# Expert rows weighted on leaving PSUM and added to the residual in DRAM by an accumulating scatter

## The chip, the cores and the metric

The kernel runs on one core of a Trainium2 chip. A core has five engines with queues of their own: TensorE (PE; its weight loads are shown as PEld), VectorE (DVE), ScalarE (ACT), GpSimd (POOL) and SyncE (SP). They meet through semaphores. Sixteen DMA engines serve the core. The metric is the device time of one execution in microseconds.

## What is computed

Two transformer blocks follow each other on 1024 tokens of width 1024, all in float32. The change lies at the seam between them: the mixture of experts that ends the first block, and the two norms behind it.

```
weight = p_group[:, None] * jax.nn.softmax(top_l, axis=-1)          # 2 experts of 32 per token
expert = (g_sel[:, None] * EXPERTS_PER_GROUP + top_i).astype(jnp.int32)
...
y = (jax.nn.silu(xb @ w_gate[e]) * (xb @ w_up[e])) @ w_down[e]      # for each expert's rows
out[token] += y * weight                                            # both rows of a token
...
x = x + hierarchical_moe(rmsnorm(x, norm2_g), ...)                  # residual
return rmsnorm(x, final_g)                                          # end of the first block
```

The second block begins with another norm of that result and its projections to queries, keys, values and a pooled branch.

## The kernel before

**Routing** (`route`). VectorE works out for each token its two experts, its place in the expert's list and its two weights `pair_w` (128 tokens by 2 slots by 8 tiles). Sixteen small matmuls of 0/1 matrices (`at_row`, `in_block`) turn these into lists, one column for each of 55 blocks of 88 rows. Adding 1024 for pairs of the second slot gives two lists from one: `row_ids` (tokens to gather) and `out_ids` (rows of a DRAM array `expert_rows` of 2048 rows, one for each pair of token and slot). GpSimd gathers block 0 within this stage, and VectorE splits two more weight units there. A barrier ends the stage.

**Experts** (`experts`). 32 blocks run, one for each expert; blocks 33 to 55 are for experts with over 88 rows, and none of them runs with these inputs. The weights of a block are 6 units of 1 MB, which SyncE loads into 13 raw slots; a slot is free again when its unit has been split. ScalarE copies a unit to reduced precision (`expert_high`), VectorE takes the remainder (`expert_rest`), both into 4 slots, and TensorE makes each product in three passes. The block's output leaves `y_ps` in two halves, one by ScalarE (`left`) and one by VectorE (`right`), into one of two `y_rows` slots. GpSimd issues for each block the gather of a block three ahead and then the store of this one, an indirect scatter to `expert_rows`; rows beyond the list's end are skipped by a bounds check. The last four raw slots lie in `res`, the place of the residual; the residual itself waits in DRAM as `mixed_residual`, and when those slots are done SyncE loads it back in 8 loads (L1781). At the end SyncE waits for the last stores and loads the first two tiles of `expert_rows`.

**Combination and norms** (first part of `project_second`). For each of 8 tiles of 128 tokens, VectorE adds the two expert rows with their weights to `res` (`put_together`, L2354), ScalarE squares and sums (L2268, L2270), VectorE scales (`final_norm`), ScalarE squares again, VectorE scales again into `poolT` (`next_norm`), TensorE transposes (L2208), and ScalarE and VectorE copy the transposed tile out of PSUM in a high part and a rest. ScalarE and VectorE also split the first four weight tiles of the projections (`ring`). From tile 3 to tile 6 TensorE runs a quarter of the first projections behind each tile's transposes. The order on each engine is written out by hand in the loops over t; the loads of `expert_rows` go through four buffers.

Of the kernel before, what the change touches and what calls it, by code (L numbers as in the profile page):

```python
# [14 lines left out]
ALU = mybir.AluOpType  # L15
# [1389 lines left out]
class CombinedRows:  # L1405


    BUF = 4

    def __init__(self, m):  # L1410
        self.m = m
        self.y = m.mixT2[:].rearrange("p (b s) d -> p b s d", s=2)
        self.y_in = [m.sem(f"y_in{i}") for i in range(self.BUF)]

    def load(self, sp, t):
        for slot in range(2):
            at = slot * SEQ + t * P
            sp.dma_start(self.y[:, t % self.BUF, slot, :], self.m.y_dram[at:at + P, :]).then_inc(self.y_in[t % self.BUF], 16)

# [19 lines left out]
def route(nc, m, A, router, weights, rows):  # L1439
# [3 lines left out]
    with ExitStack() as mem:  # L1443
# [37 lines left out]
        second = sb("second_slot", [CAP, BLOCKS])  # L1481
# [10 lines left out]
        list_mm = sem("row_list_mm")  # L1492
        ids_done = sem("row_ids_done")
# [10 lines left out]
        def _(pe):  # L1504
# [13 lines left out]
            last.then_inc(list_mm, 1)  # L1518

# [18 lines left out]
        def _(dve):  # L1538
# [22 lines left out]
            for slot in range(2):  # L1561
                step(nc.vector.tensor_scalar(place[:, slot, :], router.tokens[:], float(slot * SEQ - NOWHERE), None, ALU.add))
# [33 lines left out]
            def picked(out, table):  # L1596
# [44 lines left out]
            step(nc.vector.tensor_tensor(m.pair_w[:, 0, :], diff[:], pg[:], ALU.mult))  # L1641
            step(nc.vector.tensor_tensor(m.pair_w[:, 1, :], m.pair_w[:, 0, :], ratio[:], ALU.mult))
# [19 lines left out]
def experts(nc, m, A, weights, taken):  # L1662
# [3 lines left out]
    with ExitStack() as mem:  # L1666
# [16 lines left out]
        out_idx = sb("block_out_ids", [CAP, 1], I32)  # L1683
# [18 lines left out]
        res_back = sem("residual_back")  # L1702
# [52 lines left out]
        def left(act, s):  # L1755
            nc.scalar.activation(y[:, s, 0:BANK], ps_y[0:CAP, 0, :], ACT.Copy).then_inc(y_left, 1)

        def right(dve, s):
            nc.vector.tensor_copy(y[:, s, BANK:D], ps_y[0:CAP, 1, :]).then_inc(y_right, 1)  # L1759
# [13 lines left out]
        def _(sp):  # L1773
# [22 lines left out]
            sp.wait_ge(res_back, 16 * TT)  # L1796
# [6 lines left out]
        def put_rows(pool, s, ids):  # L1803

            pool.indirect_dma_start(m.y_dram, bass.IndirectOffsetOnAxis(ap=ids, axis=0), y[:, s, :], None,  # L1805
                                    bounds_check=2 * SEQ - 1, oob_is_err=False).then_inc(y_out[s], 16)

        @block.gpsimd
        def _(pool):
# [12 lines left out]
            for b in range(EXPERTS):  # L1822
                if b + R < EXPERTS:
                    gather(b + R)
                store(b)
            def over(j):
                pool.wait_ge(x_turned, j + EXPERTS)
                nc.gpsimd.tensor_copy(idx[:], m.row_ids[:, bass.ds(j + EXPERTS, 1)]).then_inc(over_idx, 1)
                pool.wait_ge(y_out[0], (j + EXPERTS // S) * 16)
                nc.gpsimd.tensor_copy(out_idx[:], m.out_ids[:, bass.ds(j + EXPERTS, 1)]).then_inc(over_idx, 1)  # L1830
                pool.wait_ge(over_idx, j * 2 + 2)
# [1803 lines left out]
```

## Time and profile before

| | |
|---|---|
| median of 3 runs | 2582.94 us (2579.58 to 2583.18) |
| the profiled execution | 2580.04 us, span 2578.2 us |
| granted TensorE clock, mean | 0.964 of full speed |
| busy: TensorE, VectorE, ScalarE, GpSimd | 93%, 61%, 41%, 16% |
| routing | 526 to 564 us |
| experts | 564 to 1147 us |
| combination, norms, first quarters of the projections | 1150 to 1218 us |

The page of the profile gives busy time by engine, the span in 40 slices, the DMA queues and the costliest groups of instructions. Its averages mix stages with different limits, so the stages are read apart. The traffic of GpSimd's indirect transfers is on a queue of its own (`software_dynamic`), that of SyncE's loads on another.

### The profile page before, as it was taken

The page shows a single profiled execution, that of the slowest core. Times are in us where ns is not written, and L with a number is a line of the kernel's source. Part 1 is how long each engine was busy: PE and PEld are TensorE (multiplying, and loading weights), DVE is VectorE, ACT ScalarE, POOL GpSimd, SP SyncE. Part 2 cuts the span into 40 slices and gives each one's busy share as a digit, 9 for nine tenths or more (in the row PEclk, how much of TensorE's full clock was granted, in tenths as well). Part 3 has the DMA queues.
Part 4 walks back from the last instruction along what each step waited for, and adds up shares of the span by engine and source line. Part 5 has one row for each costly group of instructions (what it writes and reads, how often), then busy time and mean ns, then how long its engine had stood idle before and what let it go on. Part 6 is the DMA issues. An engine that isn't in the chain of part 4 may idle for free. (4 is left out here: it accounts for less than half of the span.)

```text
span 2578.2 us, 28488 instructions
## 1 busy us (share of the span) xinstructions
PE 2401.0 (93%) x11160; PEld 1826.6 (71%) x11160; DVE 1581.1 (61%) x1702; ACT 1064.2 (41%) x1281; POOL 400.7 (16%) x280
## 2 busy tenths in 40 slices
PE   7999988939999999966999999998969999999998
PEld 6776556826666666646776778887858888887787
DVE  5552675368999999958213652223589998874444
ACT  4221122237777777745213741113344434433322
POOL 3110101011222222210300210000033232310000
PEclk9999998969999999987999999999989999999999
DMA  5121041289999999966310011113212222226343
GB/s 161 41 64 53 18 171 48 82 303 350 373 386 380 373 376 375 368 253 221 95 49 17 2 50 49 49 49 131 82 41 83 90 89 83 82 78 228 123 161 137
DMA packets 192965, 397.27 MB, mean 154 GB/s; under 512 B 17270, under 2 KB 120694, under 8 KB 176456
## 3 DMA queue, kind: packets, MB, share of 16 engines
q1 hardware_dynamic: 183624, 378.76, 41.5%
q0 software_dynamic: 9216, 16.80, 2.1%
q8 instruction: 83, 1.36, 0.2%
q14 instruction: 42, 0.34, 0.0%
HBM read 357.75 MB, written 47.18 MB: 157 GB/s over the span
## 5 line engine op out<-in xcount | busy, mean ns | idle before, releaser
L1398 DVE TENSOR_TENSOR expert_rest<-expert_raw,expert_high 128x2048 fp32r<-128x2048 f32 x135 | 306.0, 2290 | 43.6 <-ACT expert_high L1392 41.8
L1392 ACT ACTIVATE expert_high<-expert_raw 128x2048 fp32r<-128x2048 f32 x135 | 257.9, 1913 | 23.8 <-PE expert_up_ps L143 8.5
L141 PE MATMUL up_ps<-blocks_high,up_operand_high 128*128 128x512 f32 x616 | 241.8, 393 | 14.4 <-DVE plain_blocks_rest L3013 11.7
L143 PE MATMUL up_ps<-blocks_high,up_operand_rest 128*128 128x512 f32 x616 | 241.1, 391 | 0.0
L1805 POOL DMA_INDIRECT expert_rows<-y_rows,out_ids x32 | 85.2, 2662 | 424.6 <-DVE y_rows L1759 424.6
L141 PE MATMUL down_ps<-w_down_high,prod_high 128*128 128x512 f32 x352 | 138.4, 393 | 8.1 <-DVE w_down_rest L185 8.1
L141 PEld LDWEIGHTS up_ps<-blocks_high,up_operand_high 128*128 128x128 f32 x616 | 116.6, 189 | 40.4 <-issue 16.2
L3230 DVE TENSOR_TENSOR up_operand_rest<-res,up_operand_high 128x512 fp32r<-128x512 f32 x154 | 143.0, 940 | 3.0 <-ACT up_operand_high L3186 3.0
L1398 DVE TENSOR_TENSOR expert_rest<-res,expert_high 128x2048 fp32r<-128x2048 f32 x57 | 129.6, 2291 | 15.3 <-ACT expert_high L1392 14.7
L142 PE MATMUL down_ps<-w_down_rest,prod_high 128*128 128x512 f32 x352 | 137.9, 392 | 0.0
L142 PE MATMUL up_ps<-plain_blocks_rest,up_operand_high 128*128 128x512 f32 x352 | 137.8, 391 | 0.0
L143 PE MATMUL down_ps<-w_down_high,prod_rest 128*128 128x512 f32 x352 | 137.7, 391 | 0.0
L143 PEld LDWEIGHTS up_ps<-blocks_high,up_operand_rest 128*128 128x128 f32 x616 | 116.5, 189 | 24.3
L3144 POOL TENSOR_TENSOR res<-res 128x512 f32<-128x512 f32 x22 | 30.7, 1397 | 619.7 <-DVE plain_blocks_rest L3013 393.3
L3186 ACT ACTIVATE up_operand_high<-res 128x512 fp32r<-128x512 f32 x154 | 89.2, 622 | 83.8 <-PE up_ps L143 64.3
L1392 ACT ACTIVATE expert_high<-res 128x2048 fp32r<-128x2048 f32 x57 | 109.4, 1919 | 9.5 <-PE expert_up_ps L143 5.1
L141 PE MATMUL expert_gate_ps<-expert_high,x_high 128*88 128x512 f32 x256 | 104.0, 406 | 2.0 <-DVE x_rest L1745 2.0
L141 PE MATMUL y_ps<-expert_high,hid_high 128*88 128x512 f32 x256 | 102.5, 400 | 1.9 <-DVE y_rows L1759 1.9
L3441 DVE TENSOR_TENSOR prod_rest<-res,prod_high 128x512 fp32r<-128x512 f32 x44 | 30.5, 692 | 119.9 <-ACT prod_high L3414 119.9
L141 PE MATMUL gates_ps<-hT_high,gates_w_high 128*128 128x512 f32 x256 | 100.5, 393 | 3.3 <-DVE gates_w_rest L185 3.3
L142 PE MATMUL up_ps<-mixed_blocks_rest,up_operand_high 128*128 128x512 f32 x264 | 103.2, 391 | 0.0
L142 PE MATMUL expert_gate_ps<-expert_rest,x_high 128*88 128x512 f32 x256 | 102.2, 399 | 0.0
(432 smaller groups left out, 5915.4 us busy)
## 6 DMA issues: line engine op xcount, KB each, us to landing
expert_raw<-in_w_down_dram SPq DMA_DIRECT2D x46, 1024.0 KB, 19.0
expert_raw<-in_w_up_dram SPq DMA_DIRECT2D x45, 1024.0 KB, 19.7
expert_raw<-in_w_gate_dram SPq DMA_DIRECT2D x44, 1024.0 KB, 17.8
res<-in_w_up_dram SPq DMA_DIRECT2D x88, 256.0 KB, 4.0
res<-in_w_down_dram SPq DMA_DIRECT2D x44, 512.0 KB, 4.1
res<-in_w_gate_dram SPq DMA_DIRECT2D x20, 1024.0 KB, 22.2
res<-in_w_in_dram SPq DMA_DIRECT2D x38, 512.0 KB, 4.4
res<-in_w_up_dram SPq DMA_DIRECT2D x19, 1024.0 KB, 20.2
```

The costliest lines, as they stand in the source:

```text
L141: nc.tensor.matmul(out, w_high, x_high, start=start, stop=False)
L142: nc.tensor.matmul(out, w_high, x_rest, start=False, stop=False)
L143: return nc.tensor.matmul(out, w_rest, x_high, start=False, stop=stop)
L1392: self.nc.scalar.activation(self.high_part[:, n % SPLIT_SLOTS, :], self.raw[n % RAW_SLOTS], ACT.Copy) \
L1398: self.nc.vector.tensor_tensor(self.rest_part[:, s, :], self.raw[n % RAW_SLOTS], self.high_part[:, s, :].bitcast(F32), ALU.subtract).then_ ...
L1805: pool.indirect_dma_start(m.y_dram, bass.IndirectOffsetOnAxis(ap=ids, axis=0), y[:, s, :], None, bounds_check=2 * SEQ - 1, oob_is_err=Fals ...
L3144: nc.gpsimd.tensor_tensor(sums[:, 0], a21, a22, ALU.add).then_inc(sums_done, 1)
L3186: nc.scalar.activation(op_high[:, n % SLOTS], operand(n), ACT.Copy).then_inc(high_done, 1)
L3230: nc.vector.tensor_tensor(op_rest[:, n % SLOTS], operand(n), op_high[:, n % SLOTS].bitcast(F32), ALU.subtract) \
L3441: nc.vector.tensor_tensor(x_rest[:, n % S, :], x_raw[n % S], x_high[:, n % S, :].bitcast(F32), ALU.subtract) \
```

## The change

The weights move from the combination into the eviction, and the sum from VectorE into the store.

Routing: `row_ids` is now the list alone; `out_ids` and the second slot's offset go. A second group of 16 matmuls, of `in_block` with the pair weights as its nonzero entries, gives `row_w`, the weight of each row of each block; VectorE waits for it and copies it out. Experts: the two halves leave PSUM multiplied by the row's weight. The store is a scatter to `mixed_residual` that adds to what stands there, and since two blocks may hold the same token, each store waits until the store before it has landed. Combination: the residual's 8 reloads, the 16 loads of expert rows, their four buffers and the 16 weighted sums go; instead 8 loads bring the sums, each tile with a semaphore of its own. The loops of ScalarE and VectorE are put in a new order.

```
-            sp.dma_start(self.y[:, t % self.BUF, slot, :], self.m.y_dram[at:at + P, :]).then_inc(self.y_in[t % self.BUF], 16)
+        sp.dma_start(self.m.res[:, t, :], self.m.mixed_dram[t * P:(t + 1) * P, :]).then_inc(self.tile_in[t], 16)
...
+            pe.wait_ge(weights_placed, 1)
+            for slot in range(2):
+                for t in range(TT):
+                    last = nc.tensor.matmul(ps[0:CAP, 1, 0:BLOCKS], at_row[:, slot, t, :], in_block[:, slot, t, :],
+                                            start=(slot == 0 and t == 0), stop=(slot == 1 and t == TT - 1))
+            last.then_inc(weight_mm, 1)
...
-            step(nc.vector.tensor_scalar(second[:], listed, float(SEQ - NOWHERE), -float(SEQ), ALU.is_ge, ALU.mult))
-            nc.vector.scalar_tensor_tensor(out=m.row_ids[:], in0=listed, scalar=float(NOWHERE), in1=second[:],
-                                           op0=ALU.add, op1=ALU.add).then_inc(ids_done, 1)
-            nc.vector.tensor_scalar(m.out_ids[:], listed, float(NOWHERE), None, ALU.add)
+            nc.vector.tensor_scalar(m.row_ids[:], listed, float(NOWHERE), None, ALU.add).then_inc(ids_done, 1)
+            placed = in_block[:].rearrange("p s t c -> p (s t) c")
+            nc.vector.scalar_tensor_tensor(out=placed, in0=placed, scalar=0.0,
+                                           in1=pair_w[:].rearrange("p s t -> p (s t)").unsqueeze(2).to_broadcast(pairs + [BLOCKS]),
+                                           op0=ALU.not_equal, op1=ALU.mult).then_inc(weights_placed, 1)
+            dve.wait_ge(weight_mm, 1)
+            nc.vector.tensor_copy(m.row_w[:], ps[0:CAP, 1, 0:BLOCKS])
             dve.wait_ge(gather_begun, 1)
...
-            nc.scalar.activation(y[:, s, 0:BANK], ps_y[0:CAP, 0, :], ACT.Copy).then_inc(y_left, 1)
+            nc.scalar.activation(y[:, s, 0:BANK], ps_y[0:CAP, 0, :], ACT.Copy, scale=w).then_inc(y_left, 1)
...
-            nc.vector.tensor_copy(y[:, s, BANK:D], ps_y[0:CAP, 1, :]).then_inc(y_right, 1)
+            nc.vector.tensor_scalar(y[:, s, BANK:D], ps_y[0:CAP, 1, :], w, None, ALU.mult).then_inc(y_right, 1)
...
-                for t in range(2 * (s - OWN_SLOTS), 2 * (s - OWN_SLOTS) + 2):
-                    sp.dma_start(m.res[:, t, :], m.mixed_dram[t * P:(t + 1) * P, :]).then_inc(res_back, 16)
...
-            pool.indirect_dma_start(m.y_dram, bass.IndirectOffsetOnAxis(ap=ids, axis=0), y[:, s, :], None,
-                                    bounds_check=2 * SEQ - 1, oob_is_err=False).then_inc(y_out[s], 16)
+            pool.indirect_dma_start(m.mixed_dram, bass.IndirectOffsetOnAxis(ap=ids, axis=0), y[:, s, :], None,
+                                    bounds_check=SEQ - 1, oob_is_err=False, compute_op=ALU.add).then_inc(y_out[s], 16)
...
                 pool.wait_ge(y_right, b + 1)
-                put_rows(pool, b % S, m.out_ids[:, b:b + 1])
+                if b:
+                    pool.wait_ge(y_out[(b - 1) % S], 16 * ((b - 1) // S + 1))
+                put_rows(pool, b % S, m.row_ids[:, b:b + 1])
...
-            for n in range(2):
-                ring.load(sp, n, 0, ring_source(n), first=True)
-            for n in range(2, EARLY):
-                m.combined_rows.load(sp, n)
+            m.combined_rows.load(sp, 2)
+            ring.load(sp, 0, 0, ring_source(0), first=True)
+            for n in range(1, EARLY):
+                m.combined_rows.load(sp, n + 2)
                 ring.load(sp, n, 0, ring_source(n), first=True)
+            for t in range(EARLY + 2, TT):
+                m.combined_rows.load(sp, t)
             for t in range(TT):
-                if t + BUF < TT:
-                    sp.wait_ge(summed, t + 1)
-                    m.combined_rows.load(sp, t + BUF)
...
             for t in range(TT + 2):
-                if 1 <= t <= TT:
-                    final_norm(t - 1)
-                if t == 1:
-                    ring.rest(dve, 0, 0)
                 if t < TT:
-                    put_together(t)
+                    final_norm(t)
                 if 1 <= t <= TT:
                     next_norm(t - 1)
                 if t >= 2:
                     leave(t - 2)
-                if 2 <= t <= EARLY:
+                if 1 <= t <= EARLY:
                     ring.rest(dve, t - 1, 0)
```

VectorE's order at the end of routing, from the cast of the table of extra blocks on, before the change:

```order
L1648 CAST over_table<-over_f 1x24
L1398 TENSOR_TENSOR expert_rest<-expert_raw,expert_high 128x2048
L1653 TENSOR_SCALAR second_slot<-route_ps 88x55
L1654 SCALAR_TENSOR_TENSOR row_ids<-route_ps,second_slot 88x55
L1656 TENSOR_SCALAR out_ids<-route_ps 88x55
L1398 TENSOR_TENSOR expert_rest<-expert_raw,expert_high 128x2048 x2
```

The same place after the change:

```order
L1651 CAST over_table<-over_f 1x24
L1398 TENSOR_TENSOR expert_rest<-expert_raw,expert_high 128x2048
L1656 TENSOR_SCALAR row_ids<-route_ps 88x55
L1658 SCALAR_TENSOR_TENSOR in_block<-in_block,pair_w 128x880
L1662 COPY row_weights<-route_ps 88x55
L1398 TENSOR_TENSOR expert_rest<-expert_raw,expert_high 128x2048 x2
```

Two operations on short lists went, and two came: the weighting of `in_block`, and the copy of its product, which now stands ahead of the last two weight splits.

ScalarE's order at the start of the combination (`attT` is a scratch for squares, `norm_stats` holds sums and roots, `hT_high` is the transposed tile), before the change:

```order
L2275 ACTIVATE attT<-qkvu_ps 128x1024
L2268 ACTIVATE attT,norm_stats<-res 128x1024
L2270 ACTIVATE norm_stats<-norm_stats,eps 128x1
L181 ACTIVATE qkvu_w_high<-poolT 128x1024
L2268 ACTIVATE attT,norm_stats<-res 128x1024
L2270 ACTIVATE norm_stats<-norm_stats,eps 128x1
L2268 ACTIVATE attT,norm_stats<-res 128x1024
L2270 ACTIVATE norm_stats<-norm_stats,eps 128x1
L181 ACTIVATE qkvu_w_high<-poolT 128x1024
L181 ACTIVATE qkvu_w_high<-qkvu_raw 128x1024
L2281 ACTIVATE hT_high<-qkvu_ps 128x8x128
```

The same place after the change:

```order
L2284 ACTIVATE attT<-qkvu_ps 128x1024
L2277 ACTIVATE attT,norm_stats<-res 128x1024
L2279 ACTIVATE norm_stats<-norm_stats,eps 128x1
L181 ACTIVATE qkvu_w_high<-poolT 128x1024
L2277 ACTIVATE attT,norm_stats<-res 128x1024
L2279 ACTIVATE norm_stats<-norm_stats,eps 128x1
L2277 ACTIVATE attT,norm_stats<-res 128x1024
L2279 ACTIVATE norm_stats<-norm_stats,eps 128x1
L181 ACTIVATE qkvu_w_high<-poolT 128x1024
L2277 ACTIVATE attT,norm_stats<-res 128x1024
L2279 ACTIVATE norm_stats<-norm_stats,eps 128x1
L2277 ACTIVATE attT,norm_stats<-res 128x1024
```

Before, a tile's first square stood behind the second square of the tile ahead of it; now it stands in front of that, and the splits of the weight tiles are spread one to a tile. On VectorE the 8 pairs of L2354 are gone from the same stretch.

## Rows read from the trace of the kernel before

**Rows 1.** Busy time by stretch: us, busy (x instructions) by engine, clock, DMA share, GB/s

```profile
core 0: us, PE busy (x) PEld busy (x) DVE busy (x) ACT busy (x) POOL busy (x), PEclk, DMA share, GB/s
600.00:1100.00 500.00, 500.00 (x2387) 340.67 (x2386) 454.05 (x286) 382.74 (x285) 132.30 (x56) 1.00 1.01 374
1150.00:1186.00 36.00, 7.87 (x32) 6.27 (x32) 29.71 (x32) 21.62 (x35) 0.00 (x0) 0.50 0.95 352
1190.00:1212.00 22.00, 22.00 (x188) 22.00 (x187) 19.78 (x24) 12.91 (x24) 0.00 (x0) 1.00 0.26 99
```

**Rows 2.** The weight loads' line L1386, 600 to 620 us

```profile
DMA to landing us min/median/max: 5.2/8.1/10.2
```

**Rows 3.** The same line, 1064 to 1101 us: who waited (us, times), and landing

```profile
  ACT expert_high L1392: 2.1, 4
...
DMA to landing us min/median/max: 23.0/27.5/30.6
```

**Rows 4.** Groups by line and shape, 1140 to 1217 us: busy, mean ns, idle before

```profile
L2354 DVE SCALAR_TENSOR_TENSOR res<-mixT,pair_w,res 128x1024 f32<-128x1024 f32 x16 | 20.5, 1282 | 1.8 <-DMA mixT<-expert_rows 1.6
...
L2208 PE MATMUL qkvu_ps<-ident,poolT 128*128 128x128 f32 x64 | 12.0, 350 | 27.8 <-DVE poolT L2376 27.8
...
L2281 ACT ACTIVATE hT_high<-qkvu_ps 128x1024 fp32r<-128x1024 f32 x8 | 8.2, 1025 | 14.1 <-PE qkvu_ps L2208 14.1
```

**Rows 5.** Timeline of TensorE (start us, us, what, [idle before <-releaser]), fourth tile's transposes

```profile
1186.42 0.48 PE L2208 MATMUL qkvu_ps<-ident,poolT 128*128 128x128 f32 x1 [5.60 <-DVE poolT L2376]
```

**Rows 6.** DMA view, 607 to 1125 us: queue, then issues with median us to landing

```profile
q0 software_dynamic: 8352, 15.20, 9.3%
...
expert_rows<-y_rows,out_ids POOLq DMA_INDIRECT x30, 10.6
rows<-normed_rows,row_ids POOLq DMA_INDIRECT x28, 11.7
```

**Rows 7.** Timeline of VectorE: the split of the last expert's first unit

```profile
1107.53 2.29 DVE L1398 TENSOR_TENSOR expert_rest<-expert_raw,expert_high 128x2048 fp32r<-128x2048 f32 x1 [0.21 <-ACT expert_high L1392]
```

**Rows 8.** Timeline of TensorE: the first matmul with that unit

```profile
1114.08 0.44 PE L141 MATMUL expert_gate_ps<-expert_high,x_high 128*88 128x512 f32 x1
```

**Rows 9.** Timeline of VectorE, end of routing

```profile
548.57 1.08 DVE L1633 TENSOR_TENSOR in_block<-in_block,place 128x880 f32<-128x880 f32 x1
...
556.23 4.49 DVE L1398 TENSOR_TENSOR expert_rest<-expert_raw,expert_high 128x2048 fp32r<-128x2048 f32 x2 [0.71 <-POOLq L1526]
```

**Rows 10.** Timeline of TensorE: the list's matmuls, the first transposes of the experts

```profile
549.70 4.94 PE L1516 MATMUL route_ps<-in_block,at_row 128*88 128x55 f32 x32 [10.87 <-DVE in_block L1633]
564.94 0.41 PE L1709 MATMUL x_ps<-ident,rows 88*128 88x88 f32 x1 [10.31 <-PEq L1443]
```

**Rows 11.** Timeline of SyncE: its first load behind the barrier

```profile
563.96 0.33 SPq L1386 DMA_DIRECT2D expert_raw<-in_w_up_dram  x1
```

**Rows 12.** Timeline of VectorE: the last eviction of the experts

```profile
1139.01 0.69 DVE L1759 COPY y_rows<-y_ps 88x512 f32<-88x512 f32 x1 [6.08 <-PE y_ps L143]
```

**Rows 13.** The stores' line L1805, 1125 to 1150 us: first and last start, landing

```profile
L1805 POOL DMA_INDIRECT expert_rows<-y_rows,out_ids x2: 979/979/979, 1133.8 to 1140.6; - x2
...
DMA to landing us min/median/max: 6.5/7.6/8.7
```

**Rows 14.** The same line, 700 to 1000 us: first and last start

```profile
L1805 POOL DMA_INDIRECT expert_rows<-y_rows,out_ids x17: 2747/2784/2792, 712.7 to 994.3; - x17
```

**Rows 15.** Timeline of SyncE: the first loads behind the last landing

```profile
1147.40 0.81 SPq L1418 DMA_DIRECT2D mixT<-expert_rows  x2
```

**Rows 16.** Timeline of ScalarE, 1150 to 1162 us

```profile
1152.80 1.02 ACT L2275 ACTIVATE attT<-qkvu_ps 128x1024 f32<-128x1024 f32 x1 [1.29 <-PE qkvu_ps L2201]
...
1159.05 1.06 ACT L181 ACTIVATE qkvu_w_high<-poolT 128x1024 fp32r<-128x1024 f32 x1 [2.64 <-DMA poolT<-in_w_in_dram]
1160.01 1.04 ACT L2268 ACTIVATE attT<-res 128x1024 f32<-128x1024 f32 x1
...
1161.18 0.29 ACT L2270 ACTIVATE norm_stats<-norm_stats,eps 128x1 f32<-128x1 f32 x1
```

More of the change, by code:

```diff
@@ L1480, in route @@
         place = sb("place", [P, 2, TT])
-        second = sb("second_slot", [CAP, BLOCKS])
+        pair_w = sb("pair_w", [P, 2, TT])
         ends = sb("ends", [1, OVER, EXPERTS])
@@ L1492, in route @@
         list_mm = sem("row_list_mm")
+        weights_placed = sem("row_weights_placed")
+        weight_mm = sem("row_weight_mm")
         ids_done = sem("row_ids_done")
@@ L1753, in hid_rest_part, with left, right, weight_of @@
                 .then_inc(hid_rest_done, 1)
[L1755 to L1759 removed]
+        def left(act, s, w):
+            nc.scalar.activation(y[:, s, 0:BANK], ps_y[0:CAP, 0, :], ACT.Copy, scale=w).then_inc(y_left, 1)
+        def right(dve, s, w):
+            nc.vector.tensor_scalar(y[:, s, BANK:D], ps_y[0:CAP, 1, :], w, None, ALU.mult).then_inc(y_right, 1)
+        def weight_of(b):
+            return m.row_w[:, b:b + 1]
+        def over_weight(j):
+            return m.row_w[:, bass.ds(j + EXPERTS, 1)]
         def over_count(engine):
@@ L1929, in y_half @@
                     act.wait_ge(y_out[b % S], 16 * (b // S))
-                left(act, b % S)
+                left(act, b % S, weight_of(b))
             def ahead(n):
@@ L1970, in over @@
                 act.wait_ge(y_out[0], (j + EXPERTS // S) * 16)
-                left(act, 0)
+                left(act, 0, over_weight(j))
             over_blocks(act, count, over)
@@ L1995, in y_half @@
                     dve.wait_ge(y_out[b % S], 16 * (b // S))
-                right(dve, b % S)
+                right(dve, b % S, weight_of(b))
             def ahead(n):
@@ L2038, in over @@
                 dve.wait_ge(y_out[0], (j + EXPERTS // S) * 16)
-                right(dve, 0)
+                right(dve, 0, over_weight(j))
             over_blocks(dve, count, over)
@@ L2265, in square @@
             def square(n, t):
-                act.wait_ge((summed, normed)[n], t + 1)
+                if n:
+                    act.wait_ge(normed, t + 1)
+                else:
+                    act.wait_ge(tile_in[t], 16)
                 nc.scalar.activation(squares, m.res[:, t, :], ACT.Square, accum_out=totals[n][:, t:t + 1]).then_inc(squared[n], 1)
@@ L2276, in _ @@
             for t in range(TT + 2):
-                if 2 <= t < EARLY:
+                if t < TT:
+                    if t >= 2:
+                        act.wait_ge(squared[1], t - 1)
+                    square(0, t)
+                if 1 <= t <= TT:
+                    act.wait_ge(squared[0], min(t + 1, TT))
+                    square(1, t - 1)
+                if t < EARLY:
                     ring.high(act, t, 0, first=True)
@@ L2281, in _ @@
                     nc.scalar.activation(tile_of(hT[0], t - 2), turn_ps(t - 2), ACT.Copy).then_inc(high_done, 1)
-                if 1 <= t <= TT:
-                    square(1, t - 1)
-                if t < TT:
-                    if t:
-                        act.wait_ge(squared[1], t)
-                    square(0, t)
-                if t < 2:
-                    ring.high(act, t, 0, first=True)
             split = S
@@ L2348, in _ @@
         def _(dve):
-            def put_together(t):
-                dve.wait_ge(y_in[t % BUF], 32 * (t // BUF + 1))
-                for slot in range(2):
-                    if slot:
-                        dve.wait_ge(half_summed, t + 1)
-                    nc.vector.scalar_tensor_tensor(out=m.res[:, t, :], in0=y[:, t % BUF, slot, :],
-                                                   scalar=m.pair_w[:, slot, t:t + 1], in1=m.res[:, t, :],
-                                                   op0=ALU.mult, op1=ALU.add).then_inc((half_summed, summed)[slot], 1)
             def inverse(n, t):
```

32 lines of the change are left out of this document (10 added, 22 removed).

## The prediction

> **What bounds the kernel now.** I read the busy table by stretches first. From 600 to 1100 us, the loop over the experts, TensorE is busy for all 500 us at a granted clock of 1.00, the 16 DMA engines show a share of 1.01 and move 374 GB/s; no other long stretch has both full [rows 1]. The next question was whether the DMA engines are merely kept busy or are short. The latency of the weight loads tells it: a load of 1 MB lands 5.2 to 10.2 us after its issue at 600 to 620 us and 23.0 to 30.6 us after it from 1064 us on [rows 2, 3]. The backlog grows through the whole stage. The 13 raw slots absorb it, and only at the end does it surface: ScalarE, which splits each unit, then waits for landings, 2.1 us in four waits [rows 3]. So here a microsecond of TensorE and a microsecond of DMA engine time are worth nearly the same, and an edit that adds DMA traffic finds the reserve used up.
>
> After the loop TensorE has only 7.87 us of work between 1150 and 1186 us, at clock 0.50 [rows 1]. This is the combination and the two norms: VectorE spends 20.5 us there in 16 weighted sums, and TensorE's transposes wait 27.8 us for `poolT`, the normed tile that VectorE makes [rows 4]; those of the fourth tile start at 1186.42 us [rows 5]. From 1190 to 1212 us TensorE is full again [rows 1], since from the fourth tile on each turn also carries a quarter of the projections. The gain to be had is therefore what comes off before that fourth tile, and nothing behind it.
>
> **The change, part by part.** All terms are against the profiled execution, 2580.0 us (span 2578.2 us and 1.8 us around it); it is 2.9 us under the median of the three runs shown.
>
> *The scatter reads its destination.* A store writes 64 rows of 4 KB on average (2048 pairs over 32 blocks, 0.26 MB). Accumulating, each row must also be read from the residual. No row shows an accumulating transfer. Lower end: the read hides completely, 0. Other rows: 0.26 MB at the stage's 374 GB/s [rows 1] is 0.70 us of all engines; and the 30 scatters and 28 gathers between 607 and 1125 us take 9.3% of 16 engines for 518 us, 0.83 us each [rows 6]. Upper end: the read, the add and the write cost three passes, two more of 0.83, 1.66 us. Less than today is excluded, because the write of the same rows stays. I take 0.75, a second pass at the going rate, since it lies between the two nearest rows. The stores of blocks 0 to 28 lie ahead of the last load: 29 x 0.75 = 22 us (0 to 48).
>
> The Trainium skill (Collectives: The Full Stack, "The bandwidth ceiling: the fold count and why AG ≠ RS ≠ AR") says that a reducing transfer halves the rate, not by the add but because both sources are read through the same ring. It speaks against the change in this stage; by it a store would take twice its 0.83 us and this term would be 24 us. No trace here shows an accumulate yet.
>
> *What TensorE has in hand against that.* The first unit of the last expert is split by 1107.53 + 2.29 = 1109.8 us and used from 1114.08 us, 4.3 us later [rows 7, 8]. So the first 4 us of DMA delay do not move the end (3 to 6). The DMA waits begin only then.
>
> *Routing.* `row_ids` needs one operation instead of two, so the first gather comes a little earlier. Behind it VectorE gets the weighting of `in_block` (as L1633, 1.08 us [rows 9]), TensorE 16 more matmuls like the 16 of the list (4.94 us [rows 10]), and VectorE waits for them, with two weight splits queued behind that wait (4.49 us, which began at 556.23 us [rows 9]). VectorE would end these at 555.2 + 1.1 + 5.1 + 0.3 + 4.5 = 566.2, and the barrier falls near 566.4. It fell by 563.96 us, SyncE's first load behind it [rows 11], and TensorE started 1 us later, at 564.94 [rows 10]: +2.5 us (0 to 2.7). Since the loads behind the first 13 wait for slots that TensorE's progress frees, the whole stage moves.
>
> *Evictions.* They scale as they copy: same 88x512 shapes, 0.69 us on VectorE [rows 12]. Only the last two are followed by an idle TensorE or by the last store; 30 lie behind the 100% busy TensorE. I cost them at nothing, and 0.1 us each where the cover is gone.
>
> *The tail.* Store 31 now waits on GpSimd until store 30 has landed. Issues are at 1133.8 and 1140.6 us, landing takes 6.5 to 8.7 us [rows 13]: store 30 lands at 1142.5, so store 31 goes 1.9 us later, and I add 1.1 us for a second pass. +3 us. The lower end is -0.5, as the residual's eight reloads leave this stretch; the upper is +8, if each store takes 10.6 us as in the full stage [rows 6]. In the loop the same wait has room: 10.6 us against (994.3 - 712.7) / 16 = 17.6 us from store to store [rows 14]; queued behind it is the gather for a later block.
>
> *The combination.* Count from the first load after the last landing, B = 1147.40 us [rows 15]. Two loads there instead of four bring the barrier 0.9 us forward. The first square needs no sum and starts behind the gamma row (1152.80 + 1.02 us [rows 16]), about B+5.5. Then ScalarE, in its new order, splits a weight tile, which landed just before 1159.05 us or B+11.65 [rows 16]; with one 0.5 MB load less ahead of it and the earlier barrier I put it at B+9.8. From there ScalarE is the pace: a round is two squares with their roots (1160.01 to 1161.47, 1.5 us each), a split (1.06) [rows 16] and a copy (1.02 [rows 4]). It ends rounds 0 to 3 at B+10.8, 14.9, 20.0 and 25.0; round 4's squares end at B+28.0; behind them VectorE has the reciprocal and the two scalings left, so the fourth tile's transposes start near B+30.5. Before it was 1186.42 - 1147.40 = 39.0. Gain 8.5 us (5 if loads come late, 12 if the weight tile does not hold ScalarE). The eight reloads of the residual, which lay hidden beside the last matmuls, now stand behind the last landing on SyncE, but sixteen loads of rows go: at 352 GB/s [rows 1] 0.5 MB takes 1.5 us, a tile and a weight tile 3.0, under the 4 to 5 us of a round, so they stay hidden; without that cover each late tile costs up to 1.5 us. Behind that TensorE's own pace takes over, as before. VectorE's 20.5 us of sums are removed, but 12 of them were never on this path.
>
> Sum: 22 - 4 + 2.5 + 3 - 8.5 = +15 us: 2595 us by the profiled execution, 2598 by the median; I say **2596**.
>
> **Rivals.**
> 1. *The read of the destination hides.* The loads write SBUF, the extra read ends in HBM; were the writes into SBUF what fills the engines, it would cost nothing. Then the reserve of 4 us swallows the routing's 2.5, and the tail's 2 us stand against 8.5: 2573.5 us, or 2576 by the median, faster. Against it: 1.01 is a share of engine time, and a longer packet holds its engine. [...]
> 2. *It costs about half,* 11 us: 2584 us, no change.
> 3. *Three passes,* 48 us instead of 22: 2621 us.
> 4. *The chain of stores paces the loop.* Each store waits for the one before; if a landing takes over 18.3 us (17.6 and the 0.75 of the forecast), a block takes as long as a landing. At 20 us this adds 30 x 1.7 = 50 us: 2646 us. Today's 10.6 speaks against it [rows 6].
>
> **How the numbers follow.** Forecast 0.48 (2586 to 2610), rival 1 0.18, rival 2 0.13, rival 3 0.14, rival 4 0.07. About 0.2% (5 us) is what a measurement of this kernel can tell from no change. Slower: 0.48 + 0.14 + 0.07, less a little of the forecast's edge, 0.67; same 0.15; faster 0.18. The range leaves out rival 4, the top of rival 3 and the low third of rival 1: 2573 to 2622.
>
> **What would show it.** Between 600 us and the loop's end: the DMA share still about 1.0, load latency at its ceiling of 27 us well before 1064 us, ScalarE's waits for `in_w` loads some 15 to 20 us in all instead of 2.1, and the last y eviction some 20 us later than 1139 us. In the routing: a wait of about 5 us of VectorE for `route_ps`. In the tail: store 31 issued right behind store 30's landing. In the combination: fourth transposes 30 us behind the first load. I am wrong if the loop's last eviction moves by under 5 us (then the read hides), or if GpSimd's stores stand over 18 us apart with each issue right behind a landing (rival 4). A granted clock below 1.00 inside the loop, where waits would now open gaps, would add time that no term holds.

## The result, and the profile after

The changed kernel takes 2587.8 us (median of 15 runs, 2583.7 to 2591.6) against 2582.2 us (15 runs, 2579.6 to 2585.2): ratio 1.0021, 95% interval 1.0014 to 1.0028. It is 5.6 us slower; forecast were 14. The sign and the range held, the size did not.

The profiled execution took 2591.6 us, 3.8 above its median. 4.0 us of its distance to the kernel before arose ahead of the first changed instruction: the routing's first weight load starts at 530.04 us instead of 526.02, at a granted clock of 0.95 instead of 0.98 up to there. So every stage below is measured from its own start: the routing's first load, the first transposes of the experts, the last eviction, the first load behind the last landing (B).

Busy time by stretch, as in [rows 1]: the loop, moved by the 4 us, then the combination from its barrier to just ahead of the fourth tile, then 22 us from just behind it (us, busy (x instructions) of PE, PEld, DVE, ACT, POOL, then clock, DMA share, GB/s):

```profile
604.00:1104.00 500.00, 496.57 (x2356) 336.65 (x2355) 448.03 (x280) 377.81 (x280) 140.64 (x56) 1.00 1.01 367
1167.00:1195.00 28.00, 7.88 (x32) 6.28 (x32) 18.49 (x24) 22.70 (x41) 0.00 (x0) 0.50 0.84 283
1199.00:1221.00 22.00, 22.00 (x180) 22.00 (x180) 12.98 (x17) 9.22 (x18) 0.00 (x0) 0.96 0.51 173
```

The DMA engines are as full as before and move 367 instead of 374 GB/s, and TensorE now has gaps. In the combination VectorE falls to 18.5 us (29.7 before), and ScalarE, at 22.7 of 28, is the busy engine.

The weight loads' line, 940 to 1101 us (answers to [rows 3]), and the DMA view from 612 to 1125 us (answers to [rows 6]: queue, packets, MB, share of 16 engines; issues, median us to landing):

```profile
  ACT expert_high L1392: 40.1, 35
...
DMA to landing us min/median/max: 23.3/28.5/32.8
```

```profile
q0 software_dynamic: 8064, 14.63, 11.9%
...
mixed_residual<-y_rows,row_ids POOLq DMA_INDIRECT x29, 12.1
rows<-normed_rows,row_ids POOLq DMA_INDIRECT x28, 12.6
```

ScalarE waits 40 us for weights where it waited 2.1 [rows 3], and from 940 us on some two units in three are split as they land. (The kernel before has 2.1 us in this longer stretch too.) GpSimd's queue holds 11.9% of the engines instead of 9.3%, and a store lands in 12.1 us instead of 10.6. The stores stand 17.6 us apart up to 947 us and 15 to 22 us behind that (the last one 7). Only one store inside the loop (1042 us) waited for the landing of the one before it, so the chain of stores is not the pace.

Timelines at the ends of the stages, one engine each (start us, us, engine, line, what, [idle before <-releaser]): VectorE at the end of the routing, SyncE's first load and TensorE's first transposes behind the barrier ([rows 9 to 11]); the last eviction ([rows 12]); GpSimd's last two stores ([rows 13]); SyncE and ScalarE behind the last landing ([rows 15, 16]); the fourth tile ([rows 5]).

```profile
565.19 0.21 DVE L1662 COPY row_weights<-route_ps 88x55 f32<-88x55 f32 x1 [5.04 <-PE route_ps L1519]
565.32 4.48 DVE L1398 TENSOR_TENSOR expert_rest<-expert_raw,expert_high 128x2048 fp32r<-128x2048 f32 x2
```
```profile
570.08 0.33 SPq L1386 DMA_DIRECT2D expert_raw<-in_w_up_dram  x1
```
```profile
571.04 1.43 PE L1713 MATMUL x_ps<-ident,rows 88*128 88x88 f32 x8 [5.88 <-PEq L1438]
```
```profile
1153.86 0.75 DVE L1763 TENSOR_SCALAR y_rows<-y_ps,row_weights 88x512 f32<-88x512 f32 x1 [6.08 <-PE y_ps L143]
```
```profile
1148.80 1.57 POOL L1812 DMA_INDIRECT mixed_residual<-y_rows,row_ids  x1 [5.43 <-DMA mixed_residual<-y_rows,row_ids]
1155.85 1.56 POOL L1812 DMA_INDIRECT mixed_residual<-y_rows,row_ids  x1 [5.47 <-DMA mixed_residual<-y_rows,row_ids]
```
```profile
1162.19 0.83 SPq L1413 DMA_DIRECT2D res<-mixed_residual  x2
1167.65 0.33 SPq L2156 DMA_DIRECT2D attT<-in_final_g_dram  x1
```
```profile
1167.67 1.28 ACT L2282 ACT_TABLE_LOAD   x1 [13.13 <-PEq L1672]
```
```profile
1195.46 0.90 PE L2214 MATMUL qkvu_ps<-ident,poolT 128*128 128x128 f32 x3 [3.08 <-DVE poolT L2375]
```

Read one after the other: the experts start 41.00 us behind the routing's first load (38.92 before, so +2.1). From there to the end of the last eviction it is 583.6 us (574.8 before, +8.8). From there to the last landing, 0.2 us before B, it is 7.4 us, as before. The fourth tile starts 33.3 us behind B (39.0, so -5.7), and the first half of the projections, from tile 7 on, 65.7 us behind it (70.3, so -4.6). The line to notice is SyncE's second one: the next stage begins 5.46 us behind B, where it was 2.59. A barrier, at which all engines wait for the last one, stands between the two.

### The profile page after: what moved, and what is told of

Its sections match the earlier page's. It is cut to its first block and busy times, and to the rows that moved or that the text cites. A ratio compares the mean times of both kernels' runs of the same rounds, so it can differ in the third digit from the quotient of the medians.

```text
span 2589.8 us, 28528 instructions
## 1 busy us (share of the span) xinstructions
PE 2416.0 (93%) x11192; PEld 1837.2 (71%) x11192; DVE 1564.9 (60%) x1686; ACT 1064.7 (41%) x1281; POOL 418.6 (16%) x280
## 5 line engine op out<-in xcount | busy, mean ns | idle before, releaser
L1392 ACT ACTIVATE expert_high<-expert_raw 128x2048 fp32r<-128x2048 f32 x135 | 258.1, 1914 | 47.2 <-DMA expert_raw<-in_w_up_dram 17.6
L1812 POOL DMA_INDIRECT mixed_residual<-y_rows,row_ids x32 | 116.5, 3640 | 413.9 <-DVE y_rows L1763 394.2
L141 PE MATMUL expert_up_ps<-expert_high,x_high 128*88 128x512 f32 x256 | 101.9, 398 | 4.5 <-DVE expert_rest L1398 4.5
```

Of the source, the lines that this page charges most:

```text
L141: nc.tensor.matmul(out, w_high, x_high, start=start, stop=False)
L1392: self.nc.scalar.activation(self.high_part[:, n % SPLIT_SLOTS, :], self.raw[n % RAW_SLOTS], ACT.Copy) \
L1812: pool.indirect_dma_start(m.mixed_dram, bass.IndirectOffsetOnAxis(ap=ids, axis=0), y[:, s, :], None, bounds_check=SEQ - 1, oob_is_err=Fals ...
```

## The experiments

Stretches are from one profiled execution of each kernel; times are medians of 4 to 15 runs, and the kernel before had medians of 2580.7 to 2582.4 us when it ran beside them. e1, e9 and e13 leave out all or part of the sum of residual and expert rows. Where the verdict hangs on the loop, it is the stretch from the first transposes of the experts to the end of the last eviction. In some profiles, of either kind of store, the clock falls inside the last block (0.86 over 1135 to 1147 us in e1; the changed kernel has 1.00 over 1146 to 1156), and VectorE's wait ahead of the last eviction reads 7.6 instead of 6.1 us; 1.55 us are then taken off.

| kernel | time, us | loop, us | last weight load behind the first transposes, us | B to fourth tile, us |
|---|---|---|---|---|
| before | 2582.2 | 574.8 | 558.6 | 39.0 |
| changed | 2587.8 | 583.6 | 569.0 | 33.3 |
| e1 overwriting store | 2581.4 | 574.1 | 557.1 | 32.9 |
| e9 every second store adds | 2585.0 | 576.9 | 562.8 | 33.0 |
| e2 wait inside the body | 2584.9 | 581.2 | 568.5 | 30.1 |
| e3 copy late | 2588.5 | 582.9 | 568.7 | 33.4 |
| e8 e2 with the old order | 2591.4 | 582.6 | 570.1 | 34.9 |
| e6 before, new order | 2585.8 | 574.9 | 559.1 | 42.7 |
| e12 half rows, adding | 2597.3 | 591.9 | 576.6 | 33.2 |
| e13 half rows, overwriting | 2585.2 | 577.1 | 563.5 | 36.0 |

The landing of the last weight load is read from the DMA records of the trace.

### e1: the store overwrites

```
-                                    bounds_check=SEQ - 1, oob_is_err=False, compute_op=ALU.add).then_inc(y_out[s], 16)
+                                    bounds_check=SEQ - 1, oob_is_err=False).then_inc(y_out[s], 16)
```

> The changed kernel with a store that overwrites instead of adding; the chain of stores, the routing and the combination stay. Left out: the sum of residual and expert rows (the last writer of a row wins). Theory A, that the read of the destination holds DMA engines and this alone delayed the loop's end by 8.8 us relative to the loop's start: the last eviction comes 8 to 10 us earlier, ScalarE's waits for weight loads at the end fall back to some 2 to 4 us, time 2578 to 2580 us. As the prediction sized it (22 - 4 = 18 us): 2570 us. Rival B, that the read is free and the chain (each store waits for the one before, with a gather queued behind) delays the loop: no change, 2588 us.

2581.4 us, ratio to the kernel before 0.9994 (0.9985 to 1.0003). Timelines of TensorE (first transposes of the experts) and VectorE (last eviction):

```profile
569.62 1.14 PE L1713 MATMUL x_ps<-ident,rows 88*128 88x88 f32 x6 [5.88 <-PEq L1438]
```
```profile
1144.55 0.75 DVE L1763 TENSOR_SCALAR y_rows<-y_ps,row_weights 88x512 f32<-88x512 f32 x1 [7.63 <-PE y_ps L143]
```

The eviction ends 575.7 us behind the transposes, 574.1 with the clock's share off: theory A. The chain, the routing and the evictions are all still there, and the loop is as short as before: 9.5 us shorter than in the changed kernel. What was taken out is the read together with the add; no run here parts the two, and "the read" stands for both below. The last load lands 11.9 us earlier than in the changed kernel: 0.41 us for each of 29 reads. The same store without anything beside it, the last one, in the DMA view (e1 over 4.8 us from 1146.2, then the changed kernel over 7.2 us from 1155.8; packets, MB, share of 16 engines; the bytes read from the destination are not counted):

```profile
q0 software_dynamic: 144, 0.24, 18.1%
```
```profile
q0 software_dynamic: 144, 0.24, 22.8%
```

That is 0.87 and 1.64 us of all engines, 1.9 times, and it lands in 3.9 instead of 6.1 us. Alone the read costs 0.77 us of engine time; in the full loop it delays the loads by 0.41. The queue's share of the engines in the loop agrees more with the second figure. In e1, over 612 to 1125 us, it is:

```profile
q0 software_dynamic: 8248, 14.96, 9.2%
```

Against 11.9% in the changed kernel that is 14 us for 29 reads, or 0.5 us each.

### e9: every second store adds

```
-                put_rows(pool, b % S, m.row_ids[:, b:b + 1])
+                put_rows(pool, b % S, m.row_ids[:, b:b + 1], add=b % 2 == 1)
```

> The changed kernel with only every second store adding, the others overwriting (left out: the sums of the blocks that overwrite). Theory A, that each read of the destination delays the DMA engines by 0.41 us and the first 4 us of delay are absorbed: 14 of the 29 stores that lie ahead of the last load read, 6 - 4 = 2 us, so the stretch from the first transposes of the experts to the last eviction takes 576 to 578 us (574 to 576 with no read, 583 with all), time 2582 to 2583 us. Rival B, that there is no reserve and each read costs the loop 0.27 us: 4 us, 579 to 580 us, time 2584 to 2585 us.

The same two timelines of e9:

```profile
570.06 1.43 PE L1713 MATMUL x_ps<-ident,rows 88*128 88x88 f32 x8 [5.87 <-PEq L1438]
```
```profile
1147.72 0.75 DVE L1763 TENSOR_SCALAR y_rows<-y_ps,row_weights 88x512 f32<-88x512 f32 x1 [7.62 <-PE y_ps L143]
```

578.4 us, 576.9 with the clock's share off. The last load lands 5.7 us later than in e1, half of 11.9, so the DMA side is linear in the reads. The loop seems not to be: half the reads cost it 2.3 to 2.8 us, all of them 8.0 (mean of the changed kernel, e2, e3 and e8: 582.6; of before, e1, e6: 574.6). Measured against the same two groups, the last load is 10.8 us later with all reads (569.1 against 558.3), so 10.8 - 8.0 = 2.8 us are absorbed; against e1 alone it is 5.7 - 2.8 = 2.9 with half the reads and 11.9 - 9.5 = 2.4 with all. The stretch is theory A's, but half of 8.0 is only 1.2 to 1.7 us more than was measured, and loops of one kind differ by 0.8 to 2.4 us. The time, 2585.0 us, lies nearer to B's.

### e12 and e13: half rows

Each store becomes two scatters of 2 KB rows, adding (e12) or overwriting (e13). (The loop body is shown; the waits count 32 instead of 16.)

```
+            for half in range(2):
+                pool.indirect_dma_start(m.mixed_dram, bass.IndirectOffsetOnAxis(ap=ids, axis=0),
+                                        y[:, s, half * BANK:(half + 1) * BANK], None, element_offset=half * BANK,
```

> The changed kernel with each store split into two accumulating scatters of half rows (2 KB each): the same bytes, twice the rows. Read against e13. Theory A, that the read costs by its bytes: the last weight load lands 10 to 13 us later than in e13, as it does with whole rows (11.9). Theory B, that it costs by the row, a wait for each packet whatever its length: 20 to 26 us later than in e13, time 2600 us or more.

> As e12, but the half rows overwrite instead of adding (left out: the sum of residual and expert rows). It prices the split itself: twice the packets on the way. Both theories: at most 3 us later at the last load than with whole rows that overwrite (598.1 us from the routing's start), time 2581 to 2584 us.

2597.3 and 2585.2 us. The last load lands 13.2 us later with the add than without, near the 11.9 of whole rows and far from twice that: the read does not cost by the row. The split itself costs more than expected, 6.3 us at the last load instead of at most 3 (563.5 against 557.1). The late fourth tile of e13 is a late barrier, 8.46 us behind B. Packets and shares of the queue, e13 then e12, 612 to 1125 us:

```profile
q0 software_dynamic: 8672, 14.95, 9.4%
```
```profile
q0 software_dynamic: 12140, 14.72, 13.3%
```

The pair is less clean than it was meant to be. Only the adding stores make more packets, 3611 of 2 KB by the trace's DMA records; e13 has hardly any (38), and as many of 4 KB as whole rows give. So the 13.2 us also hold what doubled packets cost, and are an upper bound for the read. 3.9% of 513 us is 20 us, but the loads are late by 13: here the share of busy time of a queue overstates what it takes from another. With whole rows it does so by less, 14 against 11.9.

### e2: GpSimd's wait inside the body

```
-            pool.wait_ge(y_out[1], 16 * (EXPERTS // S))
             def over(j):
+                pool.wait_ge(y_out[1], 16 * (EXPERTS // S))
```

> The changed kernel with GpSimd's wait for store 31 moved from ahead of the branch over the extra blocks into their body, which does not run here; SyncE's own wait for the store stays. Theory A, that the 2.9 us by which the barrier behind the last landing came late is GpSimd's branch and end of stage, which now begin only at that landing: the barrier falls 1.7 to 2.6 us behind SyncE's first load instead of 5.5, time 2584 to 2586 us. Rival B, that the barrier is late for another reason (SyncE, loads behind one another): no change, 2588 us.

2584.9 us, ratio 1.0010 (1.0001 to 1.0019). Timelines of SyncE behind the last landing and of TensorE at the fourth tile:

```profile
1159.14 0.83 SPq L1413 DMA_DIRECT2D res<-mixed_residual  x2
1161.82 0.33 SPq L2156 DMA_DIRECT2D attT<-in_final_g_dram  x1
```
```profile
1189.23 0.69 PE L2214 MATMUL qkvu_ps<-ident,poolT 128*128 128x128 f32 x2 [3.09 <-DVE poolT L2375]
```

The next stage begins 2.68 us behind B instead of 5.46, the fourth tile at 30.1. Theory A (it had said 1.7 to 2.6), and it repeats: with the wait ahead of the branch the distance is 5.46 us in four kernels (changed, e1, e3, e9) and longer with half rows (5.76 in e12, 8.46 in e13, the last not explained); with the wait inside it is 2.67 to 2.68 in e2, e7 and e8. The time goes into an instruction at the end of GpSimd's stage, DRAIN in the trace. From the view of its line (ns, start), first in the changed kernel, then in e2:

```profile
L1672 POOLq DRAIN  x1: 5210/5210/5210, 1162.2 to 1162.2; - x1
```
```profile
L1672 POOLq DRAIN  x1: 8718/8718/8718, 1152.9 to 1152.9; - x1
```

In e2 it begins 6.1 us ahead of the last store's landing and ends 2.6 us behind it; in the changed kernel it begins only at the landing and takes 5.2 us. In the kernel before it ran as in e2 (9.2 us from 1140.5, so 2.6 us behind the landing) and was the last to reach the barrier there too. Counted from the barrier, the fourth tile starts 27.4 to 27.9 us later in all eight kernels with the new order and no sums on VectorE and plain loads (changed, e1, e2, e3, e7, e9, e12, e13), against 36.4 before.

### e3: the copy of the weights behind the splits

```
-            dve.wait_ge(weight_mm, 1)
-            nc.vector.tensor_copy(m.row_w[:], ps[0:CAP, 1, 0:BLOCKS])
             dve.wait_ge(gather_begun, 1)
             for n in (1, 2):
                 weights.rest(dve, n)
+            dve.wait_ge(weight_mm, 1)
+            nc.vector.tensor_copy(m.row_w[:], ps[0:CAP, 1, 0:BLOCKS])
```

> The changed kernel with VectorE's wait for the second group of routing matmuls, and the copy of the row weights, moved behind the last two weight splits of the routing. Theory A, that this wait delayed the start of the expert loop by 2.1 us and the loop carries the delay to its end: first transposes of the experts 2 us earlier, time 2585.5 to 2586.5 us. Rival B, that in the loop the DMA engines pace from the start, so that its end does not move: transposes 2 us earlier, but the last load lands as late as before, 2588 us.

2588.5 us, and neither theory: the transposes start only 0.5 us earlier (40.5 us behind the first load). The gather of block 0, from the view of its line (count, duration in ns min/median/max, start; then us to landing), first in the changed kernel, then in e3:

```profile
L1430 POOL DMA_INDIRECT rows<-normed_rows,row_ids x1: 1267/1267/1267, 560.2 to 560.2; - x1
...
DMA to landing us min/median/max: 7.3/7.3/7.3
```
```profile
L1430 POOL DMA_INDIRECT rows<-normed_rows,row_ids x1: 5454/5454/5454, 558.5 to 558.5; - x1
...
DMA to landing us min/median/max: 9.0/9.0/9.0
```

With VectorE's splits beside it the gather's instruction takes 5.5 instead of 1.3 us (3.2 in the kernel before, where the splits begin with it) and its rows land 1.7 us later, at 567.50; SyncE's next load follows at 567.81. In the kernel before it landed at 563.64 and the load followed at 563.96 [rows 11]. So there the end of the routing was set by this landing, not by VectorE, whose splits ended at 560.7 [rows 9]; in the changed kernel it is VectorE's (569.80, then 570.08).

### e6 and e8: the order and the sums apart

e6 is the kernel before with the new order, e8 is e2 with the old one (both loops over t as in the diff, put back or brought forward).

```
             for t in range(TT + 2):
-                if t < TT:
-                    final_norm(t)
+                if 1 <= t <= TT:
+                    final_norm(t - 1)
+                if t == 1:
+                    ring.rest(dve, 0, 0)
...
-                if 1 <= t <= EARLY:
+                if 2 <= t <= EARLY:
                     ring.rest(dve, t - 1, 0)
```

> The kernel before, with only the loops of ScalarE and VectorE in the combination in the new order; the weighted sums stay on VectorE, one tile ahead. Theory A, that the gain at the fourth tile comes from taking the sums off VectorE: with 2.6 us of sums in each round VectorE paces at 7 us or more a round, so the fourth tile starts 36 to 39 us behind the first load, time 2580 to 2583 us. Rival B, that the order alone made the gain: 30 to 31 us behind the first load, time 2574 us.

> e2 (the changed kernel with GpSimd's wait inside the body of the extra blocks) with the loops of ScalarE and VectorE in the combination back in the old order, without the sums. Theory A, that the gain comes from the sums alone and the order adds little: the fourth tile starts 31 to 34 us behind the first load, against 30.1 in e2, time 2585 to 2588 us. Rival B, that both parts are needed: 36 us or more, 2590 us.

Timelines of TensorE at the fourth tile, in e6 and then in e8:

```profile
1192.27 0.47 PE L2208 MATMUL qkvu_ps<-ident,poolT 128*128 128x128 f32 x1 [5.60 <-DVE poolT L2375]
```
```profile
1191.47 0.69 PE L2214 MATMUL qkvu_ps<-ident,poolT 128*128 128x128 f32 x2 [4.71 <-DVE poolT L2376]
```

42.7 and 34.9 us behind B, 2585.8 and 2591.4 us. Against 39.0 before, the order alone loses 3.7 us, taking off the sums alone gains 4.1, both gain 8.9 (e2). So both parts are needed for the whole gain, and the order pays only without the sums. e6 was slower than either theory said. e8 lies between the two at the fourth tile, nearer A, and at B's end in time: to the first half of the projections it needs 5.6 us more than e2 (66.9 against 61.3).

### e7 and e10: three loads earlier

e7 is e2 and e3 together with the loads of units 13 to 15 issued in the routing, e10 the kernel before with these loads.

```
-            for n in range(RAW_SLOTS):
+            for n in range(RAW_SLOTS + SPLIT_SLOTS - 1):
                 weights.load(sp, n)
```

> The changed kernel with GpSimd's wait inside the body of the extra blocks (as e2), VectorE's copy of the row weights behind the splits (as e3), and the loads of weight units 13 to 15 issued within the routing, each as soon as its slot is free, instead of behind the barrier. Theory A, that the loop's end is set by the sum of the DMA work and that the engines have a hole between the landing of the 13th unit and the first refill behind the barrier: the hole closes, the last load lands 3 to 6 us earlier relative to the routing's start than in e2, time 2579 to 2582 us. Rival B, that the engines have no such hole, or that it is filled again by the slots: 2584.5 us, as e2.

> The kernel before with the same three loads issued within the routing. Theory A, that TensorE paces the loop there and the DMA engines come short only in the last blocks: at most the 2.1 us of ScalarE's waits for landings go, 2580 to 2582 us. Rival B, that the DMA engines pace it too: 3 to 6 us less, 2577 us.

2591.7 and 2585.8 us, slower than either theory in both. The gather of block 0 in e7, as above:

```profile
L1430 POOL DMA_INDIRECT rows<-normed_rows,row_ids x1: 5462/5462/5462, 558.9 to 558.9; - x1
...
DMA to landing us min/median/max: 13.2/13.2/13.2
```

The gather shares the engines with 3 MB more of loads and lands after 13.2 us (11.1 in e10, 7.2 before), and the end of the routing waits for it: the experts start 44.7 and 42.8 us behind the first load. Nothing comes back later: behind the transposes the last load lands at 569.7 us in e7 (568.5 in e2) and at 558.4 in e10 (558.6 before). By the program each load from the 17th unit on waits for a slot that TensorE's progress frees, which would explain it; no run tests that. The hole of theory A is there (the engines move 33 GB/s over 563 to 569 us in e2), but filling it does not shorten the loop.

### e11: the add on the way in

A version without the read in the loop: plain stores as before, and per tile two accumulating loads by GpSimd into the reloaded residual.

```
+        pool.dma_start(self.m.res[:, t, :], self.m.y_dram[at:at + P, :], accum_op=ALU.add) \
+            .then_inc((self.half_in, self.tile_in)[slot][t], 16)
```

> A version without the read in the loop: rows weighted as they leave PSUM, stored plainly to the array of 2048 rows as in the kernel before, the residual reloaded beside the last matmuls as before, and the two rows of each token added to it by 16 accumulating loads of GpSimd, so that VectorE has no sums; the new order of the combination and e2's place of the wait stay. Theory A, that the loop needs only to be rid of the read, and that the combination needs only to be rid of VectorE's sums: loop 574 to 576 us from the first transposes of the experts to the last eviction, fourth tile 32 to 35 us behind the first adding load (each tile needs two loads, one after the other), time 2577 to 2580 us. Rival B, that accumulating loads are slow on the way into SBUF (a tile needs over 7 us): fourth tile 40 us or more, 2584 us or more.

2615.2 us, ratio 1.0121 (1.0104 to 1.0138). The loop is 575.8 us as hoped (574.2 with the clock's share off). The combination is not: first adding load at 1152.30, fourth tile 66.8 us later (timeline of TensorE).

```profile
1219.13 1.11 PE L2223 MATMUL qkvu_ps<-ident,poolT 128*128 128x128 f32 x4 [3.09 <-DVE poolT L2388]
```

The DMA view of this stretch, first e11 (1165 to 1200 us), then e2 (1162 to 1182 us):

```profile
DMA packets 4291, 7.52 MB, mean 215 GB/s; under 512 B 208, under 2 KB 2775, under 8 KB 4291
```
```profile
DMA packets 5471, 6.88 MB, mean 344 GB/s; under 512 B 207, under 2 KB 4303, under 8 KB 5471
```

With the engines full in both (shares of 1.05 and 1.04), 215 against 344 GB/s, bytes read back not counted. The weight tiles that ScalarE splits came 16.6 and 40.9 us after their issue where e2 has 7.9 and 7.7 (medians of two each). Rival B, with a second part that it did not name: GpSimd issues the adding loads, its DRAIN ends only at 1163.3, behind the first two of them, and the next stage begins 11.2 us behind the first. From there it is 55.6 us to the fourth tile, against 27.4 in e2.

No version run here that makes all the sums beats the kernel before; e2 is the nearest, at +2.7 us.

## Why the prediction was right or wrong

| term | predicted, us | measured, us |
|---|---|---|
| read of the destination, at the last load | 22 | 10.8 (11.9 against e1 alone) |
| absorbed by TensorE's reserve | -4 | -2.8 (2.2 to 2.9) |
| routing | +2.5 | +2.1 |
| tail | +3 | 0 |
| combination, to the first half of the projections | -8.5 | -4.6 (-9.0 in e2) |
| sum | +15 | +5.5; medians +5.6 |

The first two measured terms are the means of the section on e9. That the sum meets the medians to 0.1 us is luck: the terms are known to about 1 us, and the profiles of the two kernels alone differ by 8.8 us in the loop.

**The read, the term that failed.** "I take 0.75, since it lies between the two nearest rows" was a second pass at the going rate. It is right for a store alone (0.77) and wrong in the full loop (0.41), where it was needed: the loop's end was to move by 22 - 4 = 18 us and moved by 8 to 9.5. The time lies nearest to what rival 2 said of this term, a read at about half the cost. A queue's busy share charges it for more than others lose (20 against 13 us in e12 and e13), but that is the smaller part of the miss: by the same share the read itself holds the engines for 0.5 us in the loop. Why it holds them for less there than alone is not settled; e12 and e13 only exclude that it costs by the row.

The Trainium skill's rule that a reducing transfer halves the rate (Collectives: The Full Stack, "The bandwidth ceiling: the fold count and why AG ≠ RS ≠ AR") is stated there for the reduce step of collectives. It agrees with the store alone (1.9 times) and, less sharply, with e11 (344 to 215 GB/s). In the loop the store cost 1.24 us (0.83 + 0.41) where 0.83 stood, 1.5 times; there the measurement decides.

**Rival 1** falls with e1: the loop gives back 8 to 9.5 us when nothing but the read and its add goes. The Trainium skill (DMA: Bandwidth & Descriptors, "Where 436 GB/s comes from") lets the HBM side, not the ports into SBUF, bind transfers between HBM and SBUF; an extra read of HBM is then not free, and e1 agrees (11.9 us at the last load). **Rival 3** falls with the 0.41 us for a read. **Rival 4** falls with e1 as well, where the chain stays and the loop is short; a landing of 12.1 us leaves room in 17.6.

**The reserve** was right in kind and a little large: 2 to 3 us instead of 4, at or just under the lower end of its 3 to 6. That there is one is what e9 speaks for, where half the reads cost the loop less than half, by a margin not far above the spread.

**Routing** came out at the right size partly by luck. VectorE's wait (5.04 us, about 5 forecast) and its end were right. That VectorE's splits set the barrier in the kernel before was wrong; the gather's landing did, and moving the wait away (e3) runs into it after 0.5 us.

**The tail** was over-sized. Store 30 was to land in 8.7 us plus 1.1; it landed in 6.1, and so 0.3 us behind the last eviction. The lower end, which named the eight reloads that leave this stretch, was nearly right; that their going made the landing short is likely, but no run changes them alone.

**The combination** was right in mechanism and, without one wait, in size: the fourth tile 30.1 us behind B in e2 where 30.5 was forecast, and ScalarE the pace. What was missed is GpSimd's new wait ahead of its branch. "Two loads there instead of four bring the barrier 0.9 us forward" looked at SyncE alone. GpSimd's DRAIN set the barrier in the kernel before already, so the 0.9 us never came (2.68 us in e2, 2.59 before), and with the wait the barrier came 2.9 us later. The working had listed what is queued behind the store's wait in the loop, and not what is queued behind this one.

Of the signs to look for, the full DMA share was there, and the loads' latency at its ceiling well before 1064 us. The second one proves less than it seems to: the median reaches 28 us at about 850 us, but in the kernel before it does so at about 950. ScalarE's waits were 40 us instead of 15 to 20, for a loop that moved by half of the forecast. ScalarE is busy for 378 of 500 us and has idle time to wait in, so such waits don't measure the delay.

## What to carry to other kernels

Price an accumulating DMA by the stage it runs in, by what other transfers lose there, and measure it by running the same store without the add. When a wait is added, read on in that engine's program to its end, branches and end of stage included, and ask which barrier stands behind them. An order written for one bottleneck can cost time with another (e6), so a reorder and a removal have to be timed apart and together.

## What the runs showed of the hardware

- An accumulating DMA in a full stage: into SBUF 215 GB/s where plain loads made 344, bytes read back not counted (e11); a scatter of 0.26 MB to DRAM delayed other loads by 0.41 us more than one that overwrites (e1, e9), and not by the row (e12, e13). Alone it took 1.64 instead of 0.87 us of all engines.
- GpSimd's indirect gather took 1.3 us with VectorE idle and 5.5 us with VectorE's 128x2048 splits beside it (e3), and its rows landed 1.7 us later.
- GpSimd's DRAIN at the end of its stage ended 2.6 us behind its queue's last landing when it began ahead of it (before, e2), and took 5.2 us when it began at the landing (changed, e1, e3, e9). The barrier came 2.8 us later for it (5.46 against 2.68 us).
- Splitting an overwriting scatter into half rows delayed other loads by 6.3 us over 29 stores, with no byte more and hardly any packets of 2 KB in the trace (e13).
